# RWKV branch: a head's sums of squares with tokens on partitions, roots of 54 columns, spread back by products

## The reference

```python
w_log = -softplus(-(w0 + tanh(lw) @ w2)) - 0.5
decay = exp(-exp(w_log))               # = exp(-exp(-0.5) * sigmoid(w0 + tanh(lw) @ w2))
a = sigmoid(a0 + la @ a2);  g = sigmoid(lg) @ g2
kk = heads(k * k_k)
kk = kk / maximum(sqrt(sum(kk * kk, -1)), 1e-12)       # unit keys, one norm per head and token
k = heads(k * (1 + (a - 1) * k_a))
S = S * w_t + (S @ -kk_t) (kk_t * a_t)^T + v_t k_t^T;  out_t = S r_t      # the state, token by token
mean, var = over the 64 of a head
o = (out - mean) * rsqrt(var + 64e-5) * ln_w + ln_b
o = (o + sum(r * k * r_k, -1) * v) * g
```

## Time and profile before

| | |
|---|---|
| median of 3 runs (lowest, highest) | 2801.11 us (2799.07, 2801.87) |
| the profiled execution, its own time | 2803.04 us |
| its span, first to last instruction | 2801.4 us |
| mean granted TensorE clock over the span | 0.91 of full speed |
| TensorE busy | 2294.3 us, 82% of the span |
| VectorE busy | 1276.2 us, 46% |
| ScalarE busy | 413.8 us, 15% |
| GpSimd busy | 647.8 us, 23% |

### The profile page before, as it was taken

One profiled execution on the slowest core, in us unless ns is written; L12 is line 12 of the kernel. 1 busy time (PEld: TensorE's weight loads), 2 busy tenths in 40 slices (PEclk: granted clock), 3 DMA queues, 4 the chain that ended last, 5 costly groups with the idle time before them and its releaser, 6 DMA issues. The chain is left out here.

```text
span 2801.4 us, 46334 instructions
## 1 busy us (share of the span) xinstructions
PE 2294.3 (82%) x19075; PEld 2068.8 (74%) x19075; DVE 1276.2 (46%) x1805; ACT 413.8 (15%) x613; POOL 647.8 (23%) x582
## 2 busy tenths in 40 slices
PE   4984499847877645699459999989999999999995
PEld 3982488727634422697359999888999999999985
DVE  2347543251595841117612222214872772673652
ACT  4002222110461210003200100002100000000012
POOL 3210100001353213110011212132432332342331
PEclk6996799968999977899779999999999999999997
DMA  5140000005647769513251111031111111111112
GB/s 154 41 158 0 26 4 4 10 9 172 208 137 239 235 190 291 176 30 137 104 174 38 48 38 47 11 116 31 46 40 52 45 40 45 46 42 42 46 45 70
DMA packets 256965, 237.27 MB, mean 85 GB/s; under 512 B 22060, under 2 KB 245141, under 8 KB 255084
## 3 DMA queue, kind: packets, MB, share of 16 engines
q1 hardware_dynamic: 205792, 157.98, 18.3%
q10 hardware_dynamic: 44060, 57.57, 6.1%
q0 software_dynamic: 6912, 18.88, 2.2%
HBM read 211.10 MB, written 45.11 MB: 91 GB/s over the span
## 5 line engine op out<-in xcount | busy, mean ns | idle before, releaser
L134 PE MATMUL ps<-ml,fu_wh 128*128 128x352 f32 (+1 forms) x1248 | 410.4, 329 | 21.8 <-POOL fu_wl L128 16.7
L136 PE MATMUL ps<-mh,fu_wl 128*128 128x352 f32 (+1 forms) x1248 | 409.3, 328 | 0.0
L135 PE MATMUL ps<-mh,fu_wh 128*128 128x352 f32 (+1 forms) x1248 | 409.1, 328 | 0.0
L134 PEld LDWEIGHTS ps<-ml,fu_wh 128*128 128x128 f32 x1248 | 236.0, 189 | 23.6 <-POOL fu_wl L128 22.9
L128 POOL TENSOR_TENSOR fu_wl<-fu_wt,fu_wh 128x1024 fp32r<-128x1024 f32 (+2 forms) x84 | 191.4, 2278 | 243.3 <-DVE fu_wh L123 243.3
L135 PEld LDWEIGHTS ps<-mh,fu_wh 128*128 128x128 f32 x1248 | 236.7, 190 | 0.0
L136 PEld LDWEIGHTS ps<-mh,fu_wl 128*128 128x128 f32 x1248 | 235.7, 189 | 0.0
L134 PE MATMUL ps<-mx_l,wgh 128*128 128x352 f32 (+1 forms) x576 | 195.0, 338 | 24.0 <-DMA mx_l<-scr_xl 12.5
L136 PE MATMUL ps<-mx_h,wgl 128*128 128x352 f32 (+1 forms) x576 | 189.3, 329 | 0.0
L135 PE MATMUL ps<-mx_h,wgh 128*128 128x352 f32 (+1 forms) x576 | 189.3, 329 | 0.0
L134 PE MATMUL ps<-fu_al,fu_wh 128*128 128x384 f32 x528 | 175.6, 333 | 10.8 <-POOL fu_wl L128 7.2
(11 more groups left out here) (455 smaller groups left out, 4653.8 us busy)
## 6 DMA issues: line engine op xcount, KB each, us to landing
fu_wt<-in_w_up SPq DMA_DIRECT2D x44, 512.0 KB, 3.8
out_win_sample<-in_cache_win SPq DMA_DIRECT2D x8, 2040.0 KB, 37.3
bs_pg<-in_cache_sb_k SPq DMA_DIRECT2D x112, 128.0 KB, 3.4
bs_pg<-in_cache_sb_v SPq DMA_DIRECT2D x96, 128.0 KB, 3.9
bs_pg<-in_cache_sb_v ACTq DMA_DIRECT2D x96, 128.0 KB, 3.5
wgt<-in_w_in SPq DMA_DIRECT2D x24, 512.0 KB, 4.1
bs_pg<-in_cache_sb_k POOLq DMA_DIRECT2D x80, 128.0 KB, 3.6
fu_wt<-in_w_down SPq DMA_DIRECT2D x24, 384.0 KB, 3.4
```

What stands on the lines that cost most here:

```text
L134: nc.tensor.matmul(out, wh, xl, start=start, stop=False)
L135: nc.tensor.matmul(out, wh, xh, start=False, stop=False)
L136: return nc.tensor.matmul(out, wl, xh, start=False, stop=stop)
```

## The change

In both blocks the sum of squares of a head is no longer made by `blk` for all 64 rows alike. For each tile of 128 tokens the squares are the weights and two columns of `blk` (one per head) the moving operand, so the sums come out with tokens on partitions, 2 columns a tile, 9 tiles, 3 pairs: 54 columns for the whole block. Bound (or scale and epsilon), root and reciprocal run once on these 54 columns. The result is spread back by products: a column, repeated to 64 columns of weights, times the identity gives the factor in all 64 rows of a head. These go to PSUM, from where VectorE multiplies them into the keys, or the centred output.

Beside that, in `a_prepare`: keys times `k_k` and their squares are made by ScalarE ahead of the sigmoids (both as scaled passes of k), as is the pass with `k_a`, behind each pair's sigmoids; the decay's factor becomes the `scale` of the exponentials and its own pass goes; the first pair's exponentials no longer wait for the keys' norms; the bonus of a pair is taken from PSUM behind the next pair's work. In `a_finish` the three means, variances, gates and spreads are written out in a new order, the gates are copied out of PSUM by ScalarE, and the last step reads them from SBUF in one piece.

```diff
 def a_prepare(g):
...
+        nrm = sb("nrm", [P, PAIRS, NJ, 2])
...
+        turns = (("bs", 0), ("bs", 1), ("bc", 0), ("bs", 2), ("bc", 1), ("bc", 2))
+        bank = lambda kind, p: 3 * (turns.index((kind, p)) % 2)
+        sums = g.ps[:, 6, 0:PAIRS * NJ * 2].rearrange("t (p j h) -> t p j h", j=NJ, h=2)
...
             @block.tensor
...
+                    eng.wait_ge(s["kk"], p + 1)
+                    for j in range(NJ):
+                        mm = nc.tensor.matmul(sums[0:rows(j), p, j], ex[:, p, j * P:j * P + rows(j)], g.blk[:, 0:P:HD],
+                                              start=True, stop=True)
+                    mm.then_inc(s["ss"], 1)
                 eng.wait_ge(s["sg"], 2 * PAIRS)
+                for q, (kind, p) in enumerate(turns):
+                    if q >= 2:
+                        eng.wait_ge(s["took"], q - 1)
+                    b0 = bank(kind, p)
+                    if kind == "bs":
+                        eng.wait_ge(s["rk"], p + 1)
+                        for c, (c0, n) in enumerate(CH):
+                            mm = nc.tensor.matmul(g.ps[:, b0 + c, 0:n], g.blk, g.at[:, p, c0:c0 + n], start=True, stop=True)
+                    else:
+                        eng.wait_ge(s["rv"], 1)
+                        for j in range(NJ):
+                            n = rows(j)
+                            for h in range(2):
+                                mm = nc.tensor.matmul(g.ps[HD * h:HD * h + HD, b0 + j // 4, j % 4 * P:j % 4 * P + n],
+                                                      nrm[0:n, p, j, h:h + 1].broadcast_to([n, HD]), g.ident[0:n, 0:n],
+                                                      start=True, stop=True)
+                    mm.then_inc(s[kind], 1)
...
             @block.scalar
...
+                    nc.scalar.activation(kk[:, p, :], pa[:, K + p, :], ACT.Copy, scale=g.col("rwkv_k_k", p))
+                    nc.scalar.activation(ex[:, p, :], pa[:, K + p, :], ACT.Square, scale=g.col("rwkv_k_k", p)).then_inc(s["kk"], 1)
...
+                    nc.scalar.activation(tmp[:, p % 2, :], g.av[:, p, :], ACT.Identity, scale=g.col("rwkv_k_a", p),
+                                         bias=omk[:, p:p + 1]).then_inc(s["tm"], 1)
+                eng.wait_ge(s["nm"], 1)
+                nc.scalar.activation(nrm[:, :, :, :], nrm[:, :, :, :], ACT.Sqrt).then_inc(s["rt"], 1)
...
-                    nc.scalar.activation(ex[:, p, :], ex[:, p, :], ACT.Sqrt).then_inc(s["rt"], 1)
...
-                    eng.wait_ge(s["kn"], PAIRS)
...
+                    nc.scalar.activation(ex[:, 0, :], cu[:, p, :], ACT.Exp, scale=RATE)
...
             @block.vector
...
+                def bonus(p):
+                    eng.wait_ge(s["bs"], p + 1)
...
+                def unit_keys(p):
+                    eng.wait_ge(s["bc"], p + 1)
+                    for c, (c0, n) in enumerate(TILES):
+                        i = V_.tensor_tensor(kk[:, p, c0:c0 + n], kk[:, p, c0:c0 + n], g.ps[:, bank("bc", p) + c, 0:n], ALU.mult)
+                    i.then_inc(s["took"], 1)
...
-                    link(V_.tensor_scalar(ld[:, p, :], ld[:, p, :], -float(np.exp(-0.5)), None, ALU.mult))
...
+                    if p:
+                        bonus(p - 1)
+                    if p == 1:
+                        eng.wait_ge(s["ss"], PAIRS)
+                        V_.tensor_scalar(nrm[:, :, 0:NJ - 1, :], sums[:, :, 0:NJ - 1, :], 1e-24, None, ALU.max)
...
-                    link(V_.reciprocal(tmp[:, 1, :], ex[:, p, :]))
...
+                eng.wait_ge(s["rt"], 1)
+                V_.reciprocal(nrm[:, :, :, :], nrm[:, :, :, :]).then_inc(s["rv"], 1)
+                unit_keys(0)
+                bonus(2)
+                unit_keys(1)
+                unit_keys(2)
+                eng.wait_ge(s["took"], len(turns))
...
 def a_finish(g):
...
             @block.tensor
...
+                mean(0, 0)
+                mean(1, 3)
+                eng.wait_ge(s["om"], 1)
+                mean(2, 0)
+                variance(0)
+                eng.wait_ge(s["om"], 2)
+                gates(0, 3)
+                variance(1)
+                eng.wait_ge(s["om"], 3)
+                variance(2)
+                gates(1, 0)
+                eng.wait_ge(s["ge"], 1)
+                gates(2, 3)
+                eng.wait_ge(s["ge"], 2)
+                spread(0, 0)
+                eng.wait_ge(s["ge"], 3)
+                spread(1, 3)
+                eng.wait_ge(s["nx"], 1)
+                spread(2, 0)
...
             @block.scalar
...
+                squares(0)
+                squares(1)
+                squares(2)
+                gates(0, 3)
+                eng.wait_ge(s["ms"], 1)
+                nc.scalar.activation(nrm[:, :, :, :], nrm[:, :, :, :], ACT.Sqrt).then_inc(s["rt"], 1)
+                gates(1, 0)
+                gates(2, 3)
...
             @block.vector
...
+                eng.wait_ge(s["var"], PAIRS)
+                V_.tensor_scalar(nrm[:, :, 0:NJ - 1, :], sums[:, :, 0:NJ - 1, :], 1.0 / HD, GN_EPS, ALU.mult, ALU.add)
...
+                V_.reciprocal(nrm[:, :, :, :], nrm[:, :, :, :]).then_inc(s["rv"], 1)
...
                 for p in range(PAIRS):
...
+                    eng.wait_ge(s["bc"], p + 1)
+                    for c, (c0, n) in enumerate(TILES):
+                        ins = V_.tensor_tensor(om[:, p, c0:c0 + n], om[:, p, c0:c0 + n], g.ps[:, 3 * (p % 2) + c, 0:n], ALU.mult)
...
+                    V_.scalar_tensor_tensor(out=oa[:, p, :], in0=om[:, p, :], scalar=g.col("rwkv_ln_b", p), in1=gate[:, p, :],
+                                            op0=ALU.add, op1=ALU.mult)
```

More of the change, by code:

```diff
@@ L557, in _ @@
                 for p in range(PAIRS):
[L558 to L559 removed]
                     for half in range(2):
[L561 removed]
+                        if p:
+                            eng.wait_ge(s["sg"], 2 * (p - 1) + half + 1)
+                        at = slice(HD * half, HD * half + HD)
                         for c, (c0, n) in enumerate(CH):
[L563 to L564 removed]
+                            mm = nc.tensor.matmul(g.ps[:, 3 * half + c, 0:n], wa2[at, p * P:(p + 1) * P],
+                                                  pa[at, LWA, c0:c0 + n], start=True, stop=True)
@@ L565, in _ @@
                         mm.then_inc(s["lo"], 1)
-                eng.wait_ge(s["sg"], 2 * PAIRS)
[L567 to L577, removed]
+                    eng.wait_ge(s["kk"], p + 1)
@@ L1180, in put, with mean @@
                     mm.then_inc(s[inc], 1)
[L1181 to L1186, removed]
-                    eng.wait_ge(s["sq"], p + 1)
[L1188 to L1192, removed]
-                    eng.wait_ge(s["ms"], PAIRS)
-                    if p == 2:
-                        eng.wait_ge(s["done"], 1)
-                    put(g2[:, p * P:(p + 1) * P], g.pa[:, 10, :], 3 * (p % 2), "g")
+                def mean(p, b0):
+                    put(g.blk, oa[:, p, :], b0, "mean")
@@ new lines, in variance, with gates @@
+                def variance(p):
+                    eng.wait_ge(s["sq"], p + 1)
+                    for j in range(NJ):
+                        mm = nc.tensor.matmul(sums[0:rows(j), p, j], sq[:, p, j * P:j * P + rows(j)], g.blk[:, 0:P:HD],
+                                              start=True, stop=True)
+                    mm.then_inc(s["var"], 1)
+                def gates(p, b0):
+                    eng.wait_ge(s["w"], 16)
+                    eng.wait_ge(s["lg"], 1)
+                    put(g2[:, p * P:(p + 1) * P], g.pa[:, 10, :], b0, "g")
@@ new lines, in spread @@
+                def spread(p, b0):
+                    eng.wait_ge(s["rv"], 1)
+                    for j in range(NJ):
+                        n = rows(j)
+                        for h in range(2):
+                            mm = nc.tensor.matmul(g.ps[HD * h:HD * h + HD, b0 + j // 4, j % 4 * P:j % 4 * P + n],
+                                                  nrm[0:n, p, j, h:h + 1].broadcast_to([n, HD]), g.ident[0:n, 0:n],
+                                                  start=True, stop=True)
+                    mm.then_inc(s["bc"], 1)
```

108 lines of the change are left out of this document (53 added, 55 removed).

## The result

| | before | after |
|---|---|---|
| median (lowest, highest) of 4 runs each | 2801.49 us (2799.07, 2802.67) | 2750.40 us (2748.70, 2752.67) |
| ratio, 95% interval | | 0.9819 [0.9802, 0.9836] |
| span of the profiled execution | 2801.4 us | 2747.0 us |
| `a_prepare`, barrier to barrier | 108.29 us | 84.10 us |
| delta rule | 247.92 us | 248.53 us |

The time is 2750.4 where 2749 was forecast.

A forecast was written before the change was run, and what follows sets the result against it. VectorE was taken to bound `a_prepare` and `a_finish`, with reciprocals of 128x1088 its largest item. Savings of 26.7 and 25.5 us sum to 52.2, taking 2803.04 to 2750.8, as a median 2749; range 2740 to 2767.

The forecast's parts named there:

- the start of VectorE: `a_prepare`: VectorE starts at 219.3 and not 215.9, behind ScalarE's six new passes and a table load; 3.4 us lost.
- the wait at the first bonus: `a_prepare`: VectorE waits at pair 0's bonus from 235.1 until the first blk product releases it at 242.3; 7.2 us.
- R: `a_prepare`: end of the 54-column reciprocal, put at 252.1, the middle of 249.9 (raised clock) and 254.2 (lower clock).
- what follows the first spread: `a_prepare`: with the clock up after the first 4 us, the third spread and unit keys end at R+11.4.
- the lower walk: The step times with TensorE at the lower clock: reciprocal ends at 254.2 in `a_prepare`; `a_finish` ends at 610.2.
- a third of the way between two walks: `a_finish`: end put at 601.6, between 597.2 (upper clock) and 610.2 (lower clock); 25.5 us less.
- the upper walk: `a_finish`: the step times with TensorE at the upper clock, first spread at 584.6 and end at 597.2.
- Serial loads: Rival, sums and spreads: each weight load waits for the product before it, 0.69 us a sums record; 2842 us, chance 0.02.
- The rule of the Trainium skill: New products: a weight load overlaps running products only when its row group differs, so they would be serial.
- Halves in turn: Rival, spreads: two halves don't run side by side, each spread costs 1.9 to 3.8 us more; 2759 us, chance 0.09.
- No gain: Rival, after the barrier: something running by its own time keeps later blocks where they are; 2801 us, chance 0.02.
- The lower clock throughout: Rival, both blocks: TensorE at the lower clock becomes the bound at every hand-over; 2765 us, chance 0.15.

The follow-up runs named there:

- e5: The changed kernel with VectorE taking pair 2's work before both bonuses and the bound of the sums in `a_prepare`; 2745.9 us.
- e7: The changed kernel plus 40 unused 128x128x128 products ahead of the first spread of `a_prepare`; 2748.2 us.
- e12: The changed kernel with pair 2 before the bonuses, gates between sums, early sigmoids, first products' halves in turn and 14 filler products; 2735.2 us.
- e1: The change in `a_prepare` alone, with `a_finish` as in the kernel before; 2783.2 us, ratio 0.9926 to before.
- e6: The changed kernel with the gates of pair 1 between the sums of pairs 1 and 2 in `a_finish`; 2749.8 us.
- e11: The changed kernel with the two halves of the first products (wa2) in `a_prepare` issued in turn, piece by piece; 2753.3 us.
- e4: The changed kernel with each spread taking all tiles of one half, then all of the other, in both blocks; 2757.0 us.

## Why the prediction was right, step by step

*The size.* Forecast 52.2 us from the two blocks; measured 24.2 + 25.2 = 49.4. The profiled span fell by 54.4. The other 5.0 is in stages that the diff doesn't touch: a start 1.2 us earlier, the delta rule 0.6 longer, branch B's projection 0.8 and all behind it 3.7 shorter. That last part is the same code in all runs and lasted 2072.8 to 2085.5 us, so it is chance. By the medians the gain is 51.1, 1.7 more than the blocks gave: that 2749 is off by 1.4 and its terms by 2.8 is luck.

*`a_prepare`, 2.5 us too much.* ScalarE's six passes, the one table load, the start of VectorE, sums of 3.88 (3.84 forecast), the wait at the first bonus (6.47; 7.2 forecast), the 0.5 of the reciprocal and the 4.1 of the first spread are as forecast. R, the reciprocal's end, came 45.75 us into the block, where 252.1 is 44.75: 1.0 of the 2.5, since the middle of two levels was taken and the clock stayed at the lower one. The larger mis-sized term, 1.5, is what follows the first spread: I had the clock up behind it, but the blk product ran at 0.69 on average and took 2.95, so it is 12.9 us from R to the last products and not 11.4. With the clock up from the start it would be 10.2 (e5, e7, e12; the table counts from the reciprocal's start, 0.5 more).

*R between two levels.* R was the middle of two outcomes, and both occur: 45.7 in the change, toward the lower walk's 254.2 (46.9), and 43.1 and 43.3 in e1 and e6 with the same code, where the clock rose during the third group of products, as the text's 249.9 (42.6) had it.

*`a_finish`, 0.3 off.* VectorE's first instruction to the end of the last is 34.2 us (542.81 to 577.04); 34 was forecast, as a third of the way between two walks. The way there is a mixture too: the upper walk's steps up to the sums, the lower one's through the gates, and the first spread's release 21.8 us behind VectorE's first instruction, where the walks had 17.0 and 30.0. That a third of the way fits so well is in part luck: the same code took 1.7 us less in e11.

*The rivals.* Serial loads: 18 records in 2.15 us at the upper clock and 3.88 at the lower, 0.12 and 0.22 each against the 0.69 of that rival; it would have cost 93 us. The rule of the Trainium skill that stood beside it (TensorE: Matmul & The Clock Gate, "What overlaps and what doesn't") doesn't describe this trace: every row group is the same and loads overlap all the same. Halves in turn: excluded by e4. No gain: excluded, since the time fell by 51.1. The lower clock throughout: it came true in part, between 217 and 240 and around the first spread (247.8 to 257.5) in `a_prepare`, and from 555 to the spreads in `a_finish`.

*What stays open.* Why the clock rises behind a group of products in one execution and not in the next isn't settled. Runs with the same first instructions did both.

## What to carry to other kernels

An elementwise root or reciprocal of a row sum that was broadcast by a product of ones is worth moving ahead of the broadcast: its price goes by columns (6.95 us for 1088, 0.49 for 54), while the products that bring the factor back cost 2 to 4 us a pair and can be overlapped. Then look at what is queued behind the first wait on the new chain: here moving 8 us of ready work ahead of it brought the reciprocal forward by 6 to 8 us. And try longer products between short ones, and some work in a pause before a burst that others wait for: a burst met at the lower clock took nearly twice as long (4.09 us for 2.23). Then read the granted clock: with full products between the sums `a_finish` ran at 1.00 (e6), but with products of 64 rows between them `a_prepare` stayed at 0.50 in some executions.

## What the runs showed of the hardware

TensorE was busy for 22.56 of 23.50 us with first products, sums and blk products, and its clock stayed at 0.50 all that time (217.00 to 240.50), to rise as the second blk product began (0.96 in 240.6 to 242.4).

Products with two columns and 128x128 weights follow each other at 0.12 us a record (18 in 2.15) at the upper clock and 0.22 at the lower. Two halves with different output partitions run side by side in full (2.19 us a spread for 4.33); so do two halves with different input partitions of 64 rows, in turn (twelve records in the 4.00 us of one half's six). Half behind half the latter take 5.44, overlapping in part, and the former do not overlap.
